# A program that begins with its first feed-forward stage, with both layers of its loop written out

## What is computed

```
for l in range(DEPTH):                      # DEPTH = 2
    x = x + 0.5 * _swiglu(_rmsnorm(x, ffn1_norm[l]), ffn1_w_gate[l], ffn1_w_up[l], ffn1_w_down[l])
    h = _rmsnorm(x, mix_norm[l])
    z = h @ w_in[l]
    ...                                     # four branches; one is attention with a relative bias
    x = x + merged @ w_out[l]
    x = x + 0.5 * _swiglu(_rmsnorm(x, ffn2_norm[l]), ffn2_w_gate[l], ffn2_w_up[l], ffn2_w_down[l])
```

## Time and profile before

| | us |
|---|---|
| median of 3 runs | 2760.7 (2759.15 to 2763.48) |
| the profiled execution, its own time | 2759.07 |
| its span, first to last instruction | 2757.4 |
| bias table phase, and the first vector phase | 0 to 42.0 |
| feed-forward 1, layer 0 | 42.0 to 245.3 |
| mixer, layer 0 | 246.9 to 514.9 |
| feed-forward 2, layer 0 | 514.9 to 718.9 |
| end of loop pass, and the second vector phase | 718.9 to 727.8 |
| feed-forward 1, layer 1 | 727.8 to 931.3 |
| mixer, layer 1 | 932.5 to 1197.9 |
| second block | 1402.9 to 2757.4 |

### The profile page before, as it was taken

One profiled execution on the slowest core, in us unless ns is written; L12 is line 12 of the kernel. 1 busy time (PEld: TensorE's weight loads), 2 busy tenths in 40 slices (PEclk: granted clock), 3 DMA queues, 4 the chain that ended last, 5 costly groups with the idle time before them and its releaser, 6 DMA issues. The chain is left out here.

```text
span 2757.4 us, 34161 instructions
## 1 busy us (share of the span) xinstructions
PE 2506.6 (91%) x12924; PEld 1674.1 (61%) x12925; DVE 1225.0 (44%) x1958; ACT 859.1 (31%) x1384; POOL 43.4 (2%) x61
## 2 busy tenths in 40 slices
PE   3998999899799899989989999499999999999997
PEld 2887989688588798868867789333333333333332
DVE  2754665565475476556554464522221211211212
ACT  2444444444444454444443443111010000100101
POOL 0000000000000000000000001100000000000000
PEclk9999999999899999999999999699999999999999
DMA  5763433575375344357552124499999999999984
GB/s 222 256 209 115 151 131 117 198 263 186 143 258 206 111 148 133 121 207 251 190 146 77 56 91 130 187 421 428 429 429 428 429 428 428 429 429 428 429 340 195
DMA packets 113182, 687.46 MB, mean 249 GB/s; under 512 B 20642, under 2 KB 21922, under 8 KB 87362
## 3 DMA queue, kind: packets, MB, share of 16 engines
q1 hardware_dynamic: 105140, 651.41, 61.1%
q0 software_dynamic: 7488, 29.36, 3.0%
q10 hardware_dynamic: 432, 5.08, 0.4%
HBM read 683.70 MB, written 2.11 MB: 249 GB/s over the span
## 5 line engine op out<-in xcount | busy, mean ns | idle before, releaser
L2149 PE MATMUL ps<-wexp_all_second,con_all_whole 128*64 128x512 f32 x3168 | 705.3, 595 | 28.7 <-DMA wexp_all_second<-in_w_lin 28.6
L2149 PEld LDWEIGHTS ps<-wexp_all_second,con_all_whole 128*64 128x64 f32 x3168 | 220.5, 137 | 468.9 <-issue 395.7
L446 DVE TENSOR_TENSOR lo_first<-raw_first,hi_first 128x1024 fp32r<-128x1024 f32 x264 | 308.5, 1220 | 42.0 <-ACT hi_first L416 42.0
L241 PE MATMUL ps<-hi_first,h_hi_first 128*128 128x512 f32 x704 | 285.8, 406 | 22.1 <-DVE lo_first L446 22.1
L242 PE MATMUL ps<-lo_first,h_hi_first 128*128 128x512 f32 x704 | 280.0, 398 | 0.0
L243 PE MATMUL ps<-hi_first,h_lo_first 128*128 128x512 f32 x704 | 279.7, 397 | 0.0
L416 ACT CAST hi_first<-raw_first 128x1024 fp32r<-128x1024 f32 x264 | 260.6, 1055 | 20.6 <-DMA raw_first<-in_ffn_wgu 20.6
L241 PE MATMUL ps<-h_hi_first,w_hi_first 128*128 128x256 f32 x848 | 247.4, 292 | 3.2 <-DVE w_lo_first L891 3.2
L242 PE MATMUL ps<-h_lo_first,w_hi_first 128*128 128x256 f32 x848 | 238.5, 281 | 0.0
L243 PE MATMUL ps<-h_hi_first,w_lo_first 128*128 128x256 f32 x848 | 238.2, 281 | 0.0
L891 DVE TENSOR_TENSOR w_lo_first<-raw_first,w_hi_first 128x1024 fp32r<-128x1024 f32 x122 | 148.6, 1222 | 158.2 <-ACT w_hi_first L802 157.6
(11 more groups left out here) (430 smaller groups left out, 3387.1 us busy)
## 6 DMA issues: line engine op xcount, KB each, us to landing
wexp_all_second<-in_w_gate SPq DMA_DIRECT2D x64, 2048.0 KB, 23.0
wexp_all_second<-in_w_lin SPq DMA_DIRECT2D x64, 2048.0 KB, 25.6
wexp_all_second<-in_w_down SPq DMA_DIRECT2D x64, 2048.0 KB, 20.4
raw_first<-in_ffn_wgu SPq DMA_DIRECT2D x176, 512.0 KB, 4.9
raw_first<-in_w_mix SPq DMA_DIRECT2D x138, 512.0 KB, 3.4
raw_first<-in_ffn_wd SPq DMA_DIRECT2D x88, 512.0 KB, 5.2
raw_second<-in_w_mix SPq DMA_DIRECT2D x57, 512.0 KB, 3.3
wada_first<-in_w_ada POOLq DMA_DIRECT2D x48, 512.0 KB, 5.1
```

Of the source, the lines that this page charges most:

```text
L241: nc.tensor.matmul(out, w_hi, x_hi, start=start, stop=False, skip_group_check=True)
L446: nc.vector.tensor_tensor(lo[:, slot], raw[:, slot], hi[:, slot].bitcast(F32), ALU.subtract).then_inc(s[f"{kind}_lo"], 1)
L2149: mm = nc.tensor.matmul(dst[side(half), :], lhs(k), B.wexp[2 * "gld".index(kind) + part][:, k % 4, half * HALF:(half + 1) * HALF], start=( ...
```

## The change

`swa_table_phase` and `layer_vec_phase` are gone. The first feed-forward stage (layer 0, `first` is set) begins the program, and their work is placed inside it:

- SP loads the identity (64 KB), x as two halves with a semaphore each, the small vectors of both layers, then the first weights. The other constants follow between later groups of weights.
- ACT loads c by its own queue and makes silu of it before its first work on x; GpSimd writes it to `d_cond` and reads it back.
- PE makes one line of the bias table in each of the groups 2 to 5 in bank 7, ACT copies it into `B.sq`; SP writes the lines out after group 6's loads and reads the table back after group 7's; DVE masks it in groups 9 and 10.
- the loop over layers is a Python loop: the instructions of both layers are written out, and the addresses of all loads are fixed.

```diff
-def turn_pe(nc, s, B, x, bank):
+def turn_pe(nc, s, B, x, bank, landed=None):
     for t in range(TC):
+        if landed:
+            nc.tensor.wait_ge(landed[t], 16)
...
+    if first:
+        pool.wait_ge(s["silu"], 1)
+        pool.dma_start(B.d_cond, B.c_rows[0:1].rearrange("p a d -> p (a d)")).then_inc(s["c_out"], 16)
+        pool.wait_ge(s["c_out"], 16)
...
+            if first:
+                sp.dma_start(B.con_all[:, 0:P], first["const"][:, 0:P]).then_inc(s["ident_in"], 16)
+                for t in range(TC):
+                    sp.dma_start(x[:, t, :], first["x"][:, t, :]).then_inc(s[f"x_in{t}"], 16)
+                sp.dma_start(B.vecs, first["vec"].rearrange("l p n -> p l n")).then_inc(s["vec_in"], 16)
             load("gu", 0)
             for i in range(GROUPS):
...
+                if i == 0:
+                    sp.dma_start(B.relb, first["rel_bias"]).then_inc(s["relb_in"], 16)
+                    sp.dma_start(B.con_all[:, tables:after_tables], first["const"][:, tables:after_tables]).then_inc(s["tables_in"], 16)
+                if i == 1:
+                    sp.dma_start(B.con_all[:, P:tables], first["const"][:, P:tables]).then_inc(s["consts_in"], 16)
+                if i == 2:
+                    sp.dma_start(B.con_all[:, after_tables:], first["const"][:, after_tables:]).then_inc(s["consts_in"], 16)
+                if i == LINE_OUT_AT:
+                    sp.wait_ge(s["line_ready"], 4)
+                    sp.dma_start(B.d_line, line).then_inc(s["line_out"], 16)
+                if i == TABLE_AT:
+                    sp.wait_ge(s["line_out"], 16)
...
+            def table_line(h):
+                if h == 0:
+                    pe.wait_ge(s["tables_in"], 16)
+                    pe.wait_ge(s["relb_in"], 16)
+                else:
+                    pe.wait_ge(s["line_ready"], h)
+                nc.tensor.matmul(ps[:, 7, :], B.relb[:, h:h + 1].broadcast_to([N_BUCKETS, P]), con("bucket")[0:N_BUCKETS, :],
+                                 start=True, stop=True).then_inc(s["line_mm"], 1)
...
                 turn_hidden(i)
+                if first and LINE_AT <= i < LINE_AT + 4:
+                    table_line(i - LINE_AT)
...
+            if first:
+                act.dma_start(B.c_rows[0:1].rearrange("p a d -> p (a d)"), first["c_row"]).then_inc(s["cond_in"], 16)
+                act.wait_ge(s["cond_in"], 16)
+                nc.scalar.activation(B.c_rows[0:1], B.c_rows[0:1], ACT.Silu).then_inc(s["silu"], 1)
+                act.wait_ge(s["x_in0"], 16)
+                act.wait_ge(s["vec_in"], 16)
             square_sums(nc, s, B, x[:, 0, :], 0, 1)
...
+                if first and MASK_AT <= i < MASK_AT + 2:
+                    dve.wait_ge(s["table_in"], 16 * 4 * TC)
+                    for h in (2 * (i - MASK_AT), 2 * (i - MASK_AT) + 1):
+                        nc.vector.tensor_tensor(table_of(h), table_of(h), con("window"), ALU.add).then_inc(s["masked"], 1)
...
-            swa_table_phase(nc, B, I)
-        with nc.Fori(0, DEPTH) as l:
-            layer_vec_phase(nc, B, I, l)
+        for l in range(DEPTH):
+            B.vec, B.nsink = B.vecs[:, l], B.nsinks[:, l]
```

More of the change, by code:

```diff
@@ L252, in ffn_phase @@
             nc, ctx, B, c_rows=(P, 2, D), wada=(P, 2, D), adaprod=(P, D), adasum=(P, 2 * ADA_CTX + ADA_X))
-        ffn_program(nc, B, l, wgu, wd, gain, raw, hi, lo, sil, hid, hid_hi, hid_lo, (I["w_ada"], which))
+        ffn_program(nc, B, l, wgu, wd, gain, raw, hi, lo, sil, hid, hid_hi, hid_lo, (I["w_ada"], which),
+                    I if l == 0 and which == 0 else None)
 ADA = "c_in a_w0 a_w1 a_product a_copied "
@@ L258, with ada_pool @@
 ADA_STEPS = ADA_CTX + ADA_X
-def ada_pool(pool, nc, s, B, l, w_ada, which):
+def ada_pool(pool, nc, s, B, l, w_ada, which, first):
+    if first:
+        pool.wait_ge(s["silu"], 1)
+        pool.dma_start(B.d_cond, B.c_rows[0:1].rearrange("p a d -> p (a d)")).then_inc(s["c_out"], 16)
+        pool.wait_ge(s["c_out"], 16)
     quarters = 2 * DEPTH
@@ L317, in loads_before @@
         return i + 1 if kind == "gu" or i < last_group else GROUPS + 1
+    line = B.sq.rearrange("p k t -> p (k t)").rearrange("p (h c) -> p h c", h=4)
+    table_of = lambda h: B.swa_table[:, h * TC:(h + 1) * TC, :]
+    LINE_AT, LINE_OUT_AT, TABLE_AT, MASK_AT = 2, 6, 7, 9
     names = " ".join(f"w{n}" for n in range(6)) + " gu_hi gu_lo gu_used d_hi d_lo d_used"
[L320 removed]
+    begin = " ident_in x_in0 x_in1 vec_in cond_in silu c_out relb_in tables_in consts_in line_mm line_ready line_out table_in masked nsink_ready"
+    with phase(nc, NORM + ADA + names + " silu_done hid_done hid_turned hid_hi_done hidden_ready acc_done x_done"
+               + (begin if first else "")) as (block, s):
         @block.gpsimd
         def _(pool):
[L324 removed]
+            ada_pool(pool, nc, s, B, l, *ada, first)
         @block.sync
@@ L437, in _ @@
                 nc.scalar.copy(hid_hi.rearrange("p f t -> p (f t)"), turned_hid).then_inc(s["hid_hi_done"], 1)
+                if first and LINE_AT <= i < LINE_AT + 4:
+                    if i == LINE_AT:
+                        act.wait_ge(s["squared"], 2)
+                    act.wait_ge(s["line_mm"], i - LINE_AT + 1)
+                    nc.scalar.copy(line[:, i - LINE_AT, :], ps[:, 7, :]).then_inc(s["line_ready"], 1)
         @block.vector
@@ L447, in lower @@
                                             ALU.subtract).then_inc(s[f"{kind}_lo"], 1)
+            if first:
+                dve.wait_ge(s["vec_in"], 16)
+                nc.vector.tensor_scalar(B.nsinks, B.vecs[:, :, VEC["sink"][0]:VEC["sink"][0] + 4], -1.0, None,
+                                        ALU.mult).then_inc(s["nsink_ready"], 1)
             for k in range(KD):
@@ L477, in _ @@
             dve.wait_ge(s["a_copied"], 2)
+            if first:
+                dve.wait_ge(s["masked"], 4)
+                dve.wait_ge(s["nsink_ready"], 1)
 DEPTH_A = 3
@@ L1159, in mixer @@
         mixer_program(nc, B, l, I["w_mix"], gain)
[L1162 to L1204, removed]
-            mm.then_inc(s["line_mm"], 1)
-        @block.vector
-        def _(dve):
-            dve.wait_ge(s["line_mm"], 1)
-            nc.vector.tensor_copy(line, ps[:, 0:4, :]).then_inc(s["line_ready"], 1)
-            dve.wait_ge(s["table_in"], 16 * 4 * TC)
-            for h in range(4):
-                nc.vector.tensor_tensor(B.swa_table[:, h * TC:(h + 1) * TC, :], B.swa_table[:, h * TC:(h + 1) * TC, :],
-                                        con("window"), ALU.add).then_inc(s["masked"], 1)
-            dve.wait_ge(s["masked"], 4)
```

33 lines of the change are left out of this document (17 added, 16 removed).

## The result

| | before | after |
|---|---|---|
| median, same chip | 2762.09 us (2759.15 to 2763.77, 4 runs) | 2720.82 us (2717.71 to 2720.92, 4 runs) |
| profiled execution, own time / span | 2759.07 / 2757.4 | 2717.71 / 2715.9 |

The ratio is 0.9849, with an interval of 0.9832 to 0.9866: 41.3 us less. The forecast was 2721.0.

The account below looks back on a forecast made before the run. It took a transfer chain to bound the head and PE everything behind it. Head -36.3, pass's end -7.2 and PE's lines +3.6 sum to -39.9 us: 2719.2 against the profiled execution, 2721 as median, range 2715 to 2728.

Parts of the forecast that it names:

- What bounds the kernel: Whole program: a chain of transfers bounds the head until the first product at 49.86 us, then PE sets the pace.
- The head: Program start to first product: 49.86 becomes 13.5, vectors landing at 6.9; gain 36.3 us, ends 37.0 and 34.5.
- PE's slow start: Lower clock behind the first product: 3.2 us as before, no difference; the other case would cost 1.3 us.
- The gap between the layers: End of the loop's first pass: branch and vector phase go, saving 7.66 us; 7.2 after 0.5 lost to the clock.
- PE's lines: Four bias-table lines in groups 2 to 5 of the first stage: 3.6 us lost, other end 7.2.
- half of the time at the head, since PE is warm: Sizing of the four bias-table lines on PE: half of their 7.19 us at the head, so 3.6 us.
- What was costed at nothing: First stage: ACT's copies, DVE's masks, GpSimd's chain and the constants' loads are hidden and add no time.
- The stated margins at group 3: Gate-and-up weights behind the 8.2 us constants piece: first tile 2.7 us before it is wanted, fourth 1.9.
- Slower by the supply of instructions: Rival, layer 1 written out: PE's list comes in too slowly; 25 ns per matmul gives 2806 us; slower had 0.02.
- The thing that no step decides: Mixers: either may get or be spared a fall of PE's clock, 2.6 us up or down.
- The sum: Whole kernel: -36.3 - 7.2 + 3.6 = -39.9 us against the profiled 2759.07, with 2721 as the median.

Follow-up runs that it names:

- 4: Changed kernel with the 3.5 MB piece of constants issued ahead of the first weights, not behind group 1's: 2729.36 us, 0.9883.
- 5: Changed kernel with the small vectors of both layers loaded on ACT's queue behind c, not on SP's behind x: 2720.52 us, 0.9851.
- before_again: The kernel before, unchanged, run once more for a second profile: 2765.26 us.
- Experiment 1: The kernel before with only its loop over layers written out; table phase and vector phases stay: 2754.02 us, 0.9968.
- experiment 2: The kernel before with the loop written out and both layers' vectors loaded in the table phase, no vector phases: 2746.99 us, 0.9942.
- experiment 3: Changed kernel without PE's four bias-table products; ACT copies another array of the same size instead: 2717.06 us, 0.9837.
- experiment 6: Changed kernel with PE's four lines moved to idle places, two behind turning x, two behind the first gate-and-up: 2712.23 us, 0.9825.
- 9: Changed kernel with 6500 of the large constants' 6850 columns loaded a second time right behind, into unused memory: 2726.06 us, 0.9872.

## Why the prediction was right, step by step

**What bounds the kernel** held: head, gap and PE's lines carry -35.0, -7.8 and +4.9 of the -41.5 us between the two profiles, and a mixer with less of the lower clock (-4.1) covers the rest.

**The head.** Forecast 13.5 for the first product, measured 14.85 in one profile and 13.62 in the other, so 35.0 and 36.2 us were gained where 36.3 had been forecast. The difference is the landing of the vectors: taken as 6.9 within 6.3 to 8.7, and ACT's square began at 8.54 and 7.31. They took 6.1 us from their issue in the first, behind a second half of x that was there at 7.29 (PE's second turning) and not at 6.0. The steps behind the square were well sized. Shown by 4 and 5: the weights' loads are not on this chain, but would be with 3.5 MB ahead of them, and the vectors stand level with PE's turning of x.

**PE's slow start** behind the first product was taken as no different, 3.2 us. It was 18.01 - 14.85 = 3.16, as in the profile that was worked from. (No clock is recorded before 18.06 in this run, so it is the products' pace that shows it: 0.43 us apart, then 0.23.) But that profile's start was a short one for this kernel. In before_again PE was slow for 6.0 us, and from the first product to the end of the stage it took 197.4 us and not 195.4; experiments 1 and 2, whose head is the old one, took 197.5 each, and the changed kernel 200.33 in both of its profiles. So against the usual start of the kernel before, the new one saves some 2 us, which one profile could not show and the forecast does not have.

**The gap between the layers.** Forecast 7.66, measured 7.78. Experiment 1 shows the branch's share (4.33 with the loop's other instructions; 3.56 had been booked on it), experiment 2 the vector phase's (4.56 to 1.11, 3.45). The 0.5 us that the stage behind was to lose came to 0.2.

**PE's lines** were the term that was mis-sized: forecast 3.6 us, measured 4.9 in the stage table and 4.5 by experiment 3, inside the ends (3.6 to 7.2). The step "half of the time at the head, since PE is warm" gives 0.9 us each; PE's next product came 1.05 behind the start of a line, and the group grew by 1.24. In experiment 6 two lines behind each other took 1.98 us, 0.99 each, so a line at the higher clock is a little over half; whence the rest of the 1.24 was not tried. In the place where PE was idle anyway (6) every group behind the first took 16.8 us, and the lines were free.

**What was costed at nothing** held: ACT's copies and DVE's masks (3), the large constants (9), GpSimd's chain (DVE's first `w_ada` piece started at 35.87, right behind DVE's other work). The stated margins at group 3 rested on 8.2 us for the large piece. It took 13.2, from 43.64 to 56.8, yet the casts came on time: SP could issue the piece 4.1 us ahead of the weights, and it was in 5.4 us before their first cast. The conclusion was right with a wrong number in it.

**Slower by the supply of instructions** falls: layer 1's stages took 203.69 and 263.88 us written out, and 203.49 and 264.05 before.

**The thing that no step decides** showed itself. Of PE in the same stretch of layer 0's mixer, first in the changed kernel's first profile, with busy time, granted clock, DMA share and GB/s:

```profile
276.43:296.43 20.00, 19.57 (x152) 1.00 0.31 106
```

then in its second:

```profile
275.20:295.20 20.00, 19.56 (x139) 0.91 0.35 115
```

It is the same kernel, and the mixer took 262.63 us in the one and 265.52 in the other. So about 3 of the table's -4.1 us, and of the -41.5, come and go with the execution; against that stands the first profile's late start, 1.2. That nothing of it belongs to the change is not shown, though. In both profiles of the kernel before this mixer took 266.7 us; in the eleven of kernels with the loop written out it took 262.6 to 267.2, in the mean 264.6. Layer 1's took 264.1 and 266.6 before, 263.7 to 264.2 in the eleven. A gain of 1 to 2 us a mixer by the written-out loop would fit this, and no run separates it from chance.

**The sum.** -39.9 was forecast from one profile. The medians fell by 41.3 with the result, and by 39.4 where the changed kernel was run again (2759.94 to 2720.58). The terms as measured, without the mixer, are -35.0 to -36.2, -7.6 and +4.9: -37.7 to -38.9, and -0.6 for the other gaps. The second profiles of the two kernels lie further apart, 45.8 us (2763.6 and 2717.8): head -35.5, gap -8.0, first stage behind its first product +3.0, and -1.2 and -2.6 in the mixers. That 2721.0 met 2720.82 so closely is partly luck: lines dearer by 0.9 to 1.3 stood against a slightly better gap, shorter other gaps, the shorter slow start and the mixers, for which the sum has nothing.

## What to carry to other kernels

An edit at a program's head is worth what the first product moves (here, with PE the bound behind it), and what remains there is a race of several waits that end together: look for the second one before taking away the first (experiment 5). Work placed in the stage of the engine that sets the pace is paid even if it is small; the same work in that engine's holes was free (3, 6). Look at each table load of ACT behind a wait: a small dummy activation ahead of the wait fell into ACT's idle time, and gave more than the load's own time. A term taken from one profile can carry that execution's luck: a second profile of the kernel before would have shown a slow start twice as long.

## What had not been expected

- PE's taken branch back over a whole layer cost 3.56 us, and the gap fell by 4.33 when it went; the one not taken took 0.08.
- Where the silu had two waits, one of them stood in ACT's list ahead of the table load, and so the load stood on the chain with its 1.28 us in each feed-forward stage. Freed from it, three later stages gained 3.3 to 3.7 us each.
- An idleness of PE of 2.50 us was followed by 6.83 us at a granted clock of 0.50 (0.81 over 18 us), one of 1.17 us at the same place by 1.00 throughout. In the same kernel, PE's slow start at the head took 3.2 us in one profile and 6.0 in another.
- A transfer of 3.4 MB took 13.2 us in the middle of the stage's loads, and one of 3.25 MB right behind it 22.1.
